# A sparse gate matrix written cell by cell with indirect transfers into zeroed DRAM, instead of one-hot tiles and matmuls

## What is computed

```
def peer_ffn(xn, w_q, sub_keys, u, v):
    q = (xf @ w_q).reshape(n, PEER_HEADS, 2, PEER_DK // 2)
    s = jnp.einsum('nhpd,hpkd->nhpk', q, sub_keys).astype(jnp.float32)
    sv, si = lax.top_k(s, PEER_TOPK)
    ...
    cidx = (si[:, :, 0, :, None] * N_KEYS + si[:, :, 1, None, :]).reshape(n, PEER_HEADS, PEER_TOPK * PEER_TOPK)
    tv, tsel = lax.top_k(cand, PEER_TOPK)
    eidx = jnp.take_along_axis(cidx, tsel, axis=-1).reshape(n, PEER_HEADS * PEER_TOPK)
    g = jax.nn.softmax(tv, axis=-1).reshape(n, PEER_HEADS * PEER_TOPK).astype(xn.dtype)
    ...
    act = jax.nn.gelu(jnp.einsum('nd,ned->ne', xt, u[it]), approximate=False) * gt
    return jnp.einsum('ne,ned->nd', act, v[it])
```

## Time and profile before

| | |
|---|---|
| median of 3 runs | 2281.34 us (2273.67 to 2281.78) |
| profiled execution, its own time | 2277.62 us |
| its span in the profile | 2275.8 us |
| busy share of the span | PE 95%, weight loads 87%, DVE 71%, ACT 38%, POOL 25% |
| moved by DMA | 497.46 MB, mean 219 GB/s |

### The profile page before, as it was taken

How to read it: one execution, slowest core, us unless ns; L and a number is a source line. 1 busy time by engine, 2 the same in 40 slices (tenths; PEclk the granted TensorE clock), 3 DMA queues, 4 the chain that set the end, 5 groups by cost and what they waited for, 6 DMA issues and landing times.

```text
span 2275.8 us, 37440 instructions
## 1 busy us (share of the span) xinstructions
PE 2152.8 (95%) x14088; PEld 1972.2 (87%) x14088; DVE 1618.8 (71%) x2478; ACT 870.2 (38%) x820; POOL 575.3 (25%) x504
## 2 busy tenths in 40 slices
PE   7999867998799999999999999999999999999998
PEld 6899744798799999999999999998888888787886
DVE  6599984465543899997777777637677767767766
ACT  5333225334333433334434443433344344334333
POOL 2205900120400000004555555401122212414200
PEclk9999956799799999999999999999999999999999
DMA  6445300243244566556666666677988888898884
GB/s 241 158 164 168 120 19 19 87 161 140 75 148 134 200 203 204 203 195 211 211 214 208 216 207 224 223 264 288 359 329 327 335 343 337 312 368 337 350 300 144
DMA packets 105250, 497.46 MB, mean 219 GB/s; under 512 B 8433, under 2 KB 41345, under 8 KB 51745
## 3 DMA queue, kind: packets, MB, share of 16 engines
q1 hardware_dynamic: 57024, 390.05, 48.0%
q0 software_dynamic: 10480, 72.73, 8.5%
q10 hardware_dynamic: 37680, 33.82, 4.4%
HBM read 457.78 MB, written 37.99 MB: 218 GB/s over the span
## 4 chain that ended last, share of the span: by engine, by line
PE 63%; DVE 18%; issue 7%; DMA 6%; ACT 3%; DVEq 1%; POOL 1%; SPq 0%; ACTq 0%; POOLq 0%
PE mis L1436 12%; PE acc L1436 12%; PE acc L1200 11%; PE acc L1201 11%; PE acc L1202 11%; DVE wl L726 6%; DMA raw<-in_v 5%; DVE cacc L796 3%; PE mis L1394 1%; PE mis L1393 1%; ACT wh L436 1%; PE mis L1295 1%; DVE tsel L1002 1%; DVE top L1000 1%; PE mis L1218 1%
## 5 line engine op out<-in xcount | busy, mean ns | idle before, releaser
L726 DVE TENSOR_TENSOR wl<-raw,wh 128x2048 fp32r<-128x2048 f32 x330 | 759.5, 2304 | 321.3 <-ACT wh L436 319.8
L436 ACT ACTIVATE wh<-raw 128x2048 fp32r<-128x2048 f32 x330 | 631.4, 1915 | 866.3 <-DMA raw<-in_v 395.6
L1200 PE MATMUL acc<-xh,wh 128*128 128x256 f32 (+1 forms) x3008 | 867.2, 288 | 25.8 <-DVE wl L726 15.8
L1201 PE MATMUL acc<-xl,wh 128*128 128x256 f32 (+1 forms) x3008 | 866.7, 288 | 0.0
L1202 PE MATMUL acc<-xh,wl 128*128 128x256 f32 (+1 forms) x3008 | 861.9, 287 | 0.0
L1200 PEld LDWEIGHTS acc<-xh,wh 128*128 128x128 f32 x3008 | 572.5, 190 | 32.2 <-DVE wl L726 18.8
L1201 PEld LDWEIGHTS acc<-xl,wh 128*128 128x128 f32 x3008 | 571.3, 190 | 0.1
L1202 PEld LDWEIGHTS acc<-xh,wl 128*128 128x128 f32 x3008 | 568.2, 189 | 0.0
L1548 POOL TENSOR_SCALAR ohA<-cst,tok 128x128 fp32r<-128x128 f32 x256 | 233.5, 928 | 105.2 <-PE mis L1394 103.2
L1436 PE MATMUL mis<-wh,ah 128*128 128x512 f32 x512 | 138.8, 393 | 9.6 <-DVE wl L726 8.4
L1564 POOL DMA_INDIRECT ring<-in_ur,eidx x32 | 65.7, 2052 | 317.1 <-DVE hs L1101 277.9
(11 more groups left out here) (251 smaller groups left out, 2532.3 us busy)
## 6 DMA issues: line engine op xcount, KB each, us to landing
raw<-in_u SPq DMA_DIRECT2D x128, 1024.0 KB, 5.0
raw<-in_v SPq DMA_DIRECT2D x128, 1024.0 KB, 5.8
raw<-in_w_mix SPq DMA_DIRECT2D x28, 1024.0 KB, 4.9
raw<-in_w_out SPq DMA_DIRECT2D x16, 1024.0 KB, 4.8
raw<-in_w_pq SPq DMA_DIRECT2D x16, 1024.0 KB, 4.8
h<-hbg ACTq DMA_DIRECT2D x32, 512.0 KB
G<-gbuf ACTq DMA_DIRECT2D x16, 1024.0 KB, 7.7
hin<-h SPq DMA_DIRECT2D x32, 512.0 KB
```

Source lines behind the costliest of these rows:

```text
L436: act.activation(wh[:, n % 4], raw[:, n % 4], ACT.Copy).then_inc(hi_done, 1)
L726: dve.tensor_tensor(wl[:, n % 4], raw[:, n % 4], wh[:, n % 4].bitcast(F32), ALU.subtract).then_inc(lo_done, 1)
L1200: pe.matmul(out, wh[:, wr, b, :], mh(j), start=(j == 0), stop=False)
L1201: pe.matmul(out, wh[:, wr, b, :], ml(j), start=False, stop=False)
```

## The change

G is no longer computed by matmuls. It is zeroed in DRAM, and every pick's gate is written by itself.

- **Zeroing.** POOL clears a tile `zero` and issues 16 transfers of 1 MB from it, one for each block of G, as the slots 2, 4, ... 32 of the u stage are used.
- **Equal experts.** `gate_sums` on DVE: for each of the 2 x 128 columns of picks, one instruction over 128 x 128 compares the expert number of all picks of a token with this one and sums their gates into `gsum`. So all picks of an expert carry the full sum, and it does not matter which is written last. Four columns stand in each slot, from iteration 13 on, 64 slots.
- **Addresses.** `cells` on DVE computes once, by 7 instructions, the flat position of every pick in G.
- **Scatter.** POOL issues 256 indirect transfers, each of which writes 128 single floats, one for each token of a half. It waits for the sums once for every four.
- **What goes:** `ohA`, `ohB`, `ohL`, `gijT`, `ghl`, `tok32`, `gbuf`, the six transposes, 512 matmuls, 64 copies on ACT and 16 stores of 1 MB.
- **What moves:** the two turns for the sample group go from iterations 29 and 30 to 14 and 16. POOL's gathers stand behind its scatters. SP waits for the scatters (`scattered`) where it waited for `g_out`. G's layout is now block, partition, expert, token, so that `product` is one flat multiplication.

```
-            for b in range(2):
-                sp.wait_ge(g_out[b], 16 * U2_PAIRS)
+            for t in range(2):
+                sp.wait_ge(scattered[t], 16 * P)
...
+            def cells():
+
+                i_, j_ = (gij[:, n, 0:SU, :].rearrange("p u r -> p (u r)") for n in (1, 2))
+                own.done(dve.scalar_tensor_tensor(expert[:], i_, float(NKEYS), j_, ALU.mult, ALU.add))
...
+            def gate_sums(t, n):
+
+                at = slice(P * t, P * t + P)
+                gates = gij[:, 0, 8 * t:8 * t + 8, :].rearrange("p u r -> p (u r)")
+                for m in range(4):
+                    k = ds(P * t + 4 * n + m, 1)
+                    own.wait(0)
+                    own.done(dve.scalar_tensor_tensor(same[:], expert[:, at], expert[:, k], gates, ALU.is_equal, ALU.mult, accum_out=gsum[:, k]))
+                own.wait(0)
+                dve.sem_inc(sums_ready, 1)
...
-            with dve.Fori(0, U2_PAIRS) as i:
-                for s in range(8):
-                    lo_next(U0 + 4 * U2_0, i, s, 8)
-                    one_hots(i, s)
-                    u_evac(U2_0 + 2 * i + s // 4, s % 4)
...
+            for it in range(U2_0, 31):
+                for s in range(4):
+                    lo_next(U0, it, s)
+                    n = 4 * (it - U2_0) + s
+                    if n < 2 * P // 4:
+                        gate_sums(n // 4 % 2, 4 * (n // 8) + n % 4)
+                    u_evac(it, s)
...
-                    for t in range(4):
-                        pe.matmul(mis[:, b, P * t:P * t + P], ohA[:, b, t, :], ohB[:, b, t, :], start=True, stop=False)
-                        ins = pe.matmul(mis[:, b, P * t:P * t + P], ohA[:, b, t, :], ohL[:, b, t, :], start=False, stop=True)
-                    ins.then_inc(g_done, 1)
...
+            for b in range(NBLK):
+                pool.wait_ge(slot_used, U0 + 2 + 2 * b)
+                pool.dma_start(dr["G"][b].rearrange("p j n -> p (j n)"), zero[:]).then_inc(zero_out, 16)
...
+            for n in range(2 * P // 4):
+                pool.wait_ge(sums_ready, n + 1)
+                t, h = n // 4 % 2, n // 8
+                if n % 4 == 0 and h:
+                    pool.wait_ge(scattered[t], 16 * K16 * h)
+                for k in range(P * t + K16 * h + 4 * (n % 4), P * t + K16 * h + 4 * (n % 4) + 4):
+                    pool.indirect_dma_start(cells_of, bass.IndirectOffsetOnAxis(ap=cell[:, k:k + 1], axis=0), gsum[:, k:k + 1],
+                                            None).then_inc(scattered[t], 16)
```

More of the change, by code:

```diff
@@ L599, in u_iteration @@
                         hook(s)
[L601 to L628, removed]
             act.sem_inc(gelu_done, 1)
-            act.sem_inc(g_evac, 2)
             u_iteration(0, gelu=False)
@@ L642, in _, with xrow_evac @@
             u_iteration(U1_ITERS, hook=softmax_exp)
-            for n in range(3):
-                act.wait_ge(gt_done, n + 1)
-                act.activation(gijT[:, n, :], mis[:, n, 0:NU], ACT.Copy).then_inc(gt_out, 1)
-            act.activation(ghl[:, 0, :], mis[:, 0, 0:NU], ACT.Copy).then_inc(gt_out, 1)
-            g_pair(0, True)
-            with act.Fori(1, U2_PAIRS) as i:
-                g_pair(i, False)
-            g_out_of(U2_PAIRS - 1, 7, False)
-            g_store(U2_PAIRS - 1, 1)
+            for it in range(U2_0, XROW_IT):
+                u_iteration(it)
+            def xrow_evac(s):
+                if s == 0:
+                    act.wait_ge(xrow_turned, 1)
+                act.activation(xrow[:, 512 * s:512 * s + 512], mis[:, s, :], ACT.Copy).then_inc(xrow_out, 1)
+            u_iteration(XROW_IT, hook=xrow_evac)
             def hst_evac(s):
@@ L1089, in product @@
-                gv = gin[:].rearrange("p t (j n) -> p t j n", j=BLK)
-                dve.tensor_tensor(hv, hv, gv, ALU.mult).then_inc(prod_done, 1)
+                dve.tensor_tensor(hin[:], hin[:], gin[:], ALU.mult).then_inc(prod_done, 1)
             def act_lo(b, r):
@@ L1399, in _ @@
             ins.then_inc(hst_turned, 1)
-            for s in range(4):
-                slot(U0, U3_0, s, xh, xl, NU)
-            pe.wait_ge(xs_ready, 1)
-            pe.wait_ge(hst_copied, 4)
-            for c in range(DT):
-                ins = pe.matmul(mis[:, c // 4, P * (c % 4):P * (c % 4) + P], xs4[:, c].rearrange("p q t -> p (q t)"), ident, start=True, stop=True)
-            ins.then_inc(xrow_turned, 1)
-            with pe.Fori(U3_0 + 1, 32) as i:
+            with pe.Fori(HST_IT, 32) as i:
                 for s in range(4):
@@ L1559, in _ @@
                     pool.wait_ge(vsum_done, k - 1)
-                if g == 8:
+                pool.indirect_dma_start(ring[:, g % 2, :], None, dr["ur" if g < PICKS else "vr"],
+                                        bass.IndirectOffsetOnAxis(ap=eidx[:, k:k + 1], axis=0)).then_inc(pick_in[g % 2], 16)
+            cells_of = dr["G"].rearrange("b p j n -> (b p j n)").unsqueeze(1)
+            pool.wait_ge(zero_out, 16 * NBLK)
+            pool.wait_ge(cells_ready, 1)
+            pool.wait_ge(eidx_ready, 1)
+            for n in range(2 * P // 4):
[6 more added lines that the diff above has]
+                                            None).then_inc(scattered[t], 16)
+            pool.wait_ge(xrow_turned, 1)
+            for k in range(2 * PICKS):
+                if k == 8:
                     pool.wait_ge(hst_out, 16)
@@ L1563, in _ @@
                     pool.dma_start(sres, dr["hst"]).then_inc(hst_in, 16)
[L1564 to L1565 removed]
+                pick(k)
             pool.wait_ge(vsum_done, PICKS)
```

131 lines of the change are left out of this document (53 added, 78 removed).

## The result

The changed kernel takes 2244.39 us (median of 4 runs, 2243.16 to 2246.67), the kernel before 2281.56 us on the same chip (4 runs). The ratio is 0.984, with a 95% interval from 0.9807 to 0.9872. So it is 37 us faster (29 to 44 by the interval), where the prediction had 2272 us, 10 us faster. The profiled execution took 2243.76 us, with a span of 2242.0.

A forecast was written before the change was run, and what follows sets the result against it. PE bounds the u stage and frees 68 us, but POOL's scatters fall behind, so `product` gains only 10 us: 2281 - 10 + 1 (clock) = 2272 us. Forecast's own range 2255 to 2290, stated range 2208 to 2360.

The forecast's parts named there:

- PE's share: Gate stretch of the u stage: 1.03 us less a slot, 66 us, plus 2 us for the transposes, 68 us together.
- The zeroing costs nothing: u stage: 16 MB over 32 slots fits where DMA is at 0.57; without that cover, 48 us.
- DVE: Gate slots: four sums take 1.8 us (0.7 to 2.8), DVE has 4.5 of 5.7 us and stays below PE.
- POOL: Scatters behind the sums: pitch 1.24 to 1.37 us, starts locked out while DVE reads two SBUF operands; this decides the time.
- 3 scatters a slot: Gate slots of 5.7 us: the lock by `wl` and first sum leaves POOL three scatters where DVE delivers sums for 4.
- 40 are left: At DVE's stop before `product`, 216 of 256 scatters issued; the remaining 40 take 50 to 55 us.
- The rest of the chain: Last scatter to `product`: landing 2.5 us, then the load's 11.7 us as before; `product` at 1524.5.
- The clock: PE's restart after idling 50 us, at the lower clock, loses 1 to 2 us.
- the scatters keep up: Rival in the gate slots: four scatters a slot, PE's 68 us show in full, 2213 us; chance 0.22 (keeping up or nearly).
- the sums lock too: Rival in the gate slots: lock lasts 4.1 us, two scatters a slot, 104 left, 2355 us; chance 0.17.
- a scatter costs more than a gather: Rival on POOL: pitch 1.6 us gives 2284 us, 2.3 us gives about 2475 us; chance 0.13.
- the 4-byte pieces bind DMA: Rival on DMA engines: binds from some 150 ns a piece on, at 200 ns 2290 to 2330 us; chance 0.10.

The follow-up runs named there:

- experiment 7: G zeroed at 300 to 354 us, in the attention stage, instead of 753 to 932, against the changed kernel; 2241.86 us, ratio 0.9854 to the kernel before.
- experiment 5: `wl` cut into four operations of 512 columns, a sum behind each, in iterations 13 to 30, against the changed kernel; 2214.36 us, ratio 0.9724.
- the float subtraction behind `wl`: Changed kernel with the sums replaced by one unused float32 `tensor_tensor` of 2048 columns for each slot; 2299.81 us in one execution.
- the version with halves: `wl` in two operations of 1024 columns, two sums behind each, against the version with quarters; 2290.35 us in one execution, 2216.90 us when rerun.

## Why the prediction was right in kind and short in size

**PE's share: right.** 6.71 - 5.68 us a slot times 64 was to free 66 us, and the six transposes 2 more. From `u_evac` of iteration 12's last slot to DVE's stop it is 1467.1 - 1047.87 = 419.2 us now and 1525.75 - 1040.89 = 484.9 before, 65.7 us less: the slots' share in full, the transposes' 2 us not.

```profile
1047.87 0.42 DVE L990 TENSOR_TENSOR hbg<-acc,rstd 128x256 f32<-128x256 f32 x1
```

**"The zeroing costs nothing": wrong, 7 us.** The step asked whether DMA had room on average (0.57) and it had. But the weights must land in time, and with DMA at 0.84 and 0.86 some came late: the two rows of the stretches with 472 and 478 matmuls, which are 507 and 499 when the zeroing is elsewhere (experiment 7). So DVE stopped at 1467.1, not at 1458 (the other 2 us are the transposes'). In the changed kernel nearly all of it reaches `product`, since the scatters start later too: 6.8 us between the two kernels of experiment 7.

**DVE: right.** A sum takes 0.35 us and 0.40 from one to the next, 1.6 us a slot (forecast 1.8).

**POOL: the mechanism right, its size off.** The free pitch came as forecast, 1.26 us (1.24 to 1.37), and so did the lock: only the start, only while DVE reads two SBUF operands, and released 0.83 us before the caught one ends. The step that failed is "3 scatters a slot", "40 are left"; it was 3.3 and 17. Two things were wrong in it.

- The first sum adds nothing to the lock of `wl`: all but one of the caught scatters ended 0.82 to 0.85 us behind `wl` itself, though the row of the first sum starts 0.08 us before `wl` ends.
- I had laid out one slot as if all were alike. If `wl` came each 5.69 us, a caught scatter would end 3.1 us behind its start, the next would start at 3.4 and 4.7, and the one of 5.9 would be caught again: three a slot, with or without the first sum. But `wl` waits for `wh`, and from one `wl` to the next it was 4.3 to 8.4 us. Of the 72 distances 42 had three scatters, as forecast; all 23 of over 6.0 us had four or five. So the whole number of the layout was not the mean. Over such distances the caught one starts anywhere within the first 1.26 us of `wl`, 0.63 on average, and costs 2.29 + 0.83 - 0.96 - 0.63 = 1.53 us beyond its own time (in the trace it starts at 0.67 on average and costs 1.50). A slot then has (5.69 - 1.53) / 1.26 = 3.30 scatters; the trace has 3.3. With the first sum's 0.3 us in the lock it would be 3.06.

In numbers of the forecast: after DVE's stop it was 22 us to the end of the last scatter (1467.1 to 1489.4) instead of 52, 30 us less, of which 23 scatters fewer are 23 x 1.26 = 29; DVE's stop and with it the scatters' start came 9 us later. The 21 us between the two are the error in `product`, 1502.8 against 1524.5. Of the 28 us between 2272 and 2244 these are most; 3 us more lie behind `product` (1.7 us shorter, where 1 us longer was forecast), and the rest is that the profiled execution of the kernel before was 3 to 4 us faster than its median.

**The rest of the chain: right.** From the last scatter's start to `product` 14.35 us (1488.46 to 1502.81; forecast 1.0 + 2.5 + 11.7 = 15.2, of which the landing took 1.3 instead of 2.5). The clock: PE idled 27.66 us, and the grant was 0.50, the lower of its two levels. The stretches of PE at rest and at its restart:

```profile
1490.00:1503.00 13.00, 0.00 (x0) 0.00 (x0) 0.19 (x1) 0.00 (x0) 1.68 (x2) 0.50 0.89 359
...
1505.00:1510.00 5.00, 2.31 (x11) 2.31 (x12) 5.00 (x6) 4.86 (x3) 0.00 (x0) 0.50 0.37 154
1510.00:1515.00 5.00, 5.00 (x36) 5.00 (x36) 5.00 (x5) 0.65 (x1) 0.94 (x1) 0.78 0.62 210
```

11 matmuls in the first 2.31 us instead of 19, and 36 in the next 5 instead of 42: 14 x 0.119 = 1.7 us lost; 1 to 2 was forecast.

**The rivals.** That the scatters keep up happened only where `wl` was cut or half of them left out; the time given for it, 2213, is what those versions take (2213 to 2217). That the sums lock too: they do, but not in a row with `wl`, as this rival had it. The scatter that `wl` held goes in before the first sum, the next one comes with the start of the fourth, and one caught in a sum loses little (0.12 us in the changed kernel, 1.07 against 0.96). That only the fourth is met, and at its start, was luck of the lengths. That a scatter costs more than a gather: 0.96 us each, and the gather behind the last scatter has 0.99. That the 4-byte pieces bind DMA: the gate stretch has DMA at 0.63 with PE at 100%, and while the last 17 went out alone, at their full pitch, the share was 0.09:

```profile
1467.00:1490.00 23.00, 13.03 (x110) 12.82 (x108) 0.13 (x1) 1.92 (x1) 17.51 (x19) 0.89 0.09 31
```

The Trainium skill (DMA: Bandwidth & Descriptors, "Specifications") has transfers below 512 bytes do a read-modify-write; whether they do can't be seen here, only that at 128 pieces each 1.26 us the scatters kept their pitch.

## What to carry to other kernels

When work moves to an engine that another one can lock out, compute its rate as (period - mean loss) / pitch, with the loss from a random phase, where the distances between the locks vary by as much as the pitch, and not by laying out one slot as if all were alike (in the quarters of experiment 5 the starts were not random: 46 of the 124 that fell in a quarter stood 0.06 to 0.08 us behind its start); then compare the rate with the one that is needed (here 3.3 against 3.6), since a stall is the difference times all slots. If it falls a little short, cut the locking operation in pieces before anything is taken away from the slow engine: the same DVE work in two or four pieces gave 21 to 26 us here by the ratios, 27 to 30 by the times. A transfer that is hidden on average still costs where the weights have to land in time.

## What the runs showed of the hardware that was not expected

- What a caught scatter loses follows the length of DVE's operation; that it is caught does not. At 512, 1024 and 2048 columns (0.69, 1.22 and 2.29 us) two SBUF operands held a scatter that started inside, in subtraction as `tensor_tensor` and as `scalar_tensor_tensor`, with the scalar a constant or in SBUF, and writing either float type. At 128 columns with an accumulator (0.35 us) they did too, if it started 0.09 us or more into the operation: six in the kernel with quarters, each ending 0.83 us behind the sum. So the loss is what is left of DVE's operation, plus 0.83, less 0.96 us. The Trainium skill (SBUF — State Buffer, "Who interferes with whom") says that `tensor_tensor` does not stall descriptor generation; the scatters of up to 3.09 us that ended 0.83 us behind `wl` were held by one all the same. Whether their generation or the reading of their addresses waited, the trace does not tell.
- `u_evac`, 128x256 in 0.42 us with one operand in PSUM and one in SBUF, held none: over all these kernels 104 scatters started 0.08 to 0.25 us into one, and the longest took 0.96 us.
- In the changed kernel the four scatters that started less than 0.04 us behind a `wl` went first, and `wl` took up to 0.07 us longer (2.36 instead of 2.29); from 0.05 us on they were caught.
- A scatter of 128 single floats takes POOL as long as a gather of 128 rows of 8 KB, 0.96 us, with 0.30 us to the next; the pitch of 1.26 us held for 17 in a row.
- Two locks back to back are not always one. In the kernel before a gather waited through both (4.94 us); with the float subtraction behind `wl` a scatter got in between them (1204.35, ended at 1206.33 while the second ran). The kernel before has both kinds itself: the gather of 1925.26 got in between `wl` and `product` after 2.75 us. What makes the difference is open.
- One execution in these had PE break off for 9 to 17 us at a time without a wait, and took 73 us more (2290 against 2217 us for the same program). Taken alone it would have condemned the version with halves.
